# Router logits with transposed x as the stationary side

## What is computed

```python
h = modulate(rms_norm(x, norm2_g[i]), sh2, sc2)        # (256, 1024)
scores = sigmoid(h @ router_w)                         # (256, 16)
biased = scores + router_bias
# best group by the sum of its two best, best two experts in it, weights = scores / their sum
for e in range(16):
    y = y + gates[:, e:e+1] * (silu(h @ w1[e]) * (h @ w3[e]) @ w2[e])
x = x + g2 * y
```

## Time and profile before

| | |
|---|---|
| median of 3 runs | 1086.7 us (1086.18 to 1087.69) |
| span of the profiled execution | 1085.1 us |
| TensorE busy (PE) | 1046.2 us, 96% |
| weight loads (PEld) | 574.4 us, 53% |
| VectorE busy | 469.5 us, 43% |
| ScalarE busy | 174.3 us, 16% |
| read from HBM | 330.54 MB |

### The profile page before, as it was taken

How to read it: one execution, slowest core, us unless ns; L and a number is a source line. 1 busy time by engine, 2 the same in 40 slices (tenths; PEclk the granted TensorE clock), 3 DMA queues, 4 the chain that set the end, 5 groups by cost and what they waited for, 6 DMA issues and landing times.

```text
span 1085.1 us, 17591 instructions
## 1 busy us (share of the span) xinstructions
PE 1046.2 (96%) x7533; PEld 574.4 (53%) x7533; DVE 469.5 (43%) x1024; ACT 174.3 (16%) x340; POOL 20.4 (2%) x40
## 2 busy tenths in 40 slices
PE   7999999999999999999999999999999999999885
PEld 3688667654446344443448866765444634444322
DVE  3477696644125422352235769660112532222114
ACT  4021101310014113101121110031001410111102
POOL 3000000000000000000000000000000000000000
PEclk9999999999999999999999999999999999999998
DMA  9997846268953999999999884525665399999992
GB/s 305 391 386 256 304 157 214 79 216 321 413 229 135 411 420 415 421 421 420 421 398 368 295 301 166 185 89 194 252 266 217 137 422 421 420 421 421 421 420 118
DMA packets 90917, 332.78 MB, mean 307 GB/s; under 512 B 5020, under 2 KB 5355, under 8 KB 66005
## 3 DMA queue, kind: packets, MB, share of 16 engines
q1 hardware_dynamic: 87905, 323.56, 76.3%
q0 software_dynamic: 2048, 6.09, 1.6%
q10 hardware_dynamic: 884, 1.97, 0.6%
HBM read 330.54 MB, written 1.05 MB: 306 GB/s over the span
## 4 chain that ended last, share of the span: by engine, by line
PE 82%; DMA 7%; DVE 6%; SPq 3%; issue 1%; ACT 1%; DVEq 0%
PE bank L735 80%; DMA ring<-in_moe_w_dram 3%; SPq L665 2%; DMA wide<-in_moe_w_dram 2%; DMA ring<-in_w_ada_dram 2%; PE bank L1007 1%; PE bank L1175 1%; DVE wide L1586 0%; DVE area L1779 0%; DVE wide L1784 0%; DVE area L1782 0%; PE bank L1093 0%; DVE area L1781 0%; DVE area L1780 0%; PE bank L788 0%
## 5 line engine op out<-in xcount | busy, mean ns | idle before, releaser
L735 PE MATMUL bank<-ring,hT 128*32 128x512 f32 (+3 forms) x1808 | 311.6, 555 | 4.4 <-DMA ring<-in_moe_w_dram 1.8
L735 PE MATMUL bank<-hT,ring 128*32 128x256 f32 (+1 forms) x2112 | 214.1, 380 | 0.2 <-DVE hT L1620 0.2
L735 PEld LDWEIGHTS bank<-ring,hT 128*32 128x32 f32 (+2 forms) x1808 | 129.0, 136 | 152.8 <-issue 149.1
L735 PEld LDWEIGHTS bank<-hT,ring 128*32 128x32 f32 (+1 forms) x2112 | 158.7, 132 | 55.3 <-issue 8.7
L735 PE MATMUL bank<-area 32*64 32x64 f32 (+5 forms) x648 | 96.1, 363 | 0.5 <-ACT area L1468 0.5
L735 PE MATMUL bank<-ring,area 128*32 128x512 f32 x664 | 81.8, 594 | 0.5 <-ACT area L1468 0.5
L2051 DVE TENSOR_TENSOR area<-bank,area 128x512 f32<-128x512 f32 x14 | 9.7, 691 | 148.4 <-PE bank L735 148.4
L735 PEld LDWEIGHTS bank<-area 32*64 32x64 f32 (+4 forms) x648 | 43.8, 145 | 54.2 <-issue 52.2
L735 PE MATMUL bank<-wide,hT 128*32 128x512 f32 x368 | 65.9, 603 | 2.8 <-DMA ring<-in_moe_w_dram 1.4
L735 PE MATMUL bank<-ring,wide 128*128 128x512 f32 (+1 forms) x192 | 64.0, 597 | 0.8 <-DMA ring<-in_w_ada_dram 0.8
L1586 DVE SCALAR_TENSOR_TENSOR area<-ring,wide,area 128x512 f32<-128x512 f32 x84 | 63.1, 751 | 2.5
(11 more groups left out here) (266 smaller groups left out, 895.3 us busy)
## 6 DMA issues: line engine op xcount, KB each, us to landing
ring<-in_moe_w_dram SPq DMA_DIRECT2D x135, 1024.0 KB, 14.5
ring<-in_w_in_dram SPq DMA_DIRECT2D x26, 2048.0 KB, 11.4
ring<-in_w_ada_dram SPq DMA_DIRECT2D x24, 2048.0 KB, 14.2
wide<-in_moe_w_dram SPq DMA_DIRECT2D x33, 1024.0 KB, 12.2
cst<-in_moe_w_dram SPq DMA_DIRECT2D x13, 1024.0 KB, 14.9
area<-in_moe_w_dram SPq DMA_DIRECT2D x11, 1024.0 KB, 14.5
ring<-in_w_out_dram SPq DMA_DIRECT2D x4, 2048.0 KB, 8.0
ring<-in_w_br_h_dram SPq DMA_DIRECT2D x4, 1536.0 KB, 7.9
```

The source lines that it names most:

```text
L735: return pe.matmul(dst, lhsT, rhs, start=start, stop=stop, skip_group_check=True)
```

## The change

The partial sums, ScalarE's copy of them and the fold are taken out. `route(tt)` now makes, for each of the eight pieces, one matmul with the transposed x (128 tokens) as the stationary side and `routerA[:, k, :]` (16 columns, no zeros) as the moving side, all eight added up in 16 columns of bank 2. The result has the tokens on the rows. The wait for ScalarE's half of `xT` stands ahead of the fifth matmul. `routerA` is stored without padding and is no longer filled with zeros. The fillers stay as they are.

```diff
-        turned_in = region(ND * 32 + SEQ)
-        routerA = turned_in[:, 0:ND * 32].rearrange("p (k e) -> p k e", k=ND)
-        part = turned_in[:, ND * 32:].rearrange("p (t s) -> p t s", t=NT)
+        routerA = region(ND * NE).rearrange("p (k e) -> p k e", k=ND)
...
                 def route(tt):
-                    for r in range(2):
-                        if r == 0:
-                            pe.wait_ge(v_ra, L + 1)
-                            pe.wait_ge(v_xT, L * NT + tt + 1)
-                        else:
+                    pe.wait_ge(v_ra, L + 1)
+                    pe.wait_ge(v_xT, L * NT + tt + 1)
+                    for k in range(ND):
+                        if k == 4:
                             pe.wait_ge(a_xT, L * NT + tt + 1)
-                        for j in range(4):
-                            k = 4 * r + j
-                            last = mm(bank[tt][32 * j:32 * j + 32, 0:P], routerA[:, k, :], xT[:, tt, k, :],
-                                      r == 0, r == 1)
-                    last.then_inc(p_part, 1)
+                        last = mm(bank[2][:, tt * NE:(tt + 1) * NE], xT[:, tt, k, :], routerA[:, k, :],
+                                  k == 0, k == ND - 1)
+                    if tt == NT - 1:
+                        last.then_inc(p_lg, 1)
...
                 route(1)
-                for tt in range(NT):
-                    pe.wait_ge(a_part, L * NT + tt + 1)
-                    last = mm(bank[2][:, tt * NE:(tt + 1) * NE], part[:, tt, :], fold, True, True)
-                last.then_inc(p_lg, 1)
                 keep_clock(3, 9)
...
-                def keep_part(tt):
-                    sc.wait_ge(p_part, L * NT + tt + 1)
-                    sc.activation(part[:, tt, :], bank[tt][:, 0:P], ACT.Copy).then_inc(a_part, 1)
...
                 keep_xT(0)
-                keep_part(0)
...
                 keep_xT(1)
-                keep_part(1)
...
-                        link(dv.memset(routerA, 0.0))
-                        dv.tensor_tensor(routerA[:, :, 0:NE], router[:, :, :],
+                        dv.tensor_tensor(routerA, router[:, :, :],
```

More of the change, by code:

```diff
@@ L455, in trunk_kernel @@
         a_xT = sem("a_xT")
-        p_part = sem("p_part")
-        a_part = sem("a_part")
         v_lg = sem("v_lg")
```

## The result

The changed kernel takes 1089.45 us (median of 12 runs, 1088.47 to 1090.54), the kernel before beside it 1086.91 us (12 runs, 1086.18 to 1088.04): 2.54 us more, a ratio of 1.002 with a 95% interval of 1.0013 to 1.0027. The forecast was 1089.4 us. The profiled execution has a span of 1087.8 us.

A forecast was written before the change was run, and what follows sets the result against it. TensorE, on 82% of the chain that ended last, bounds the kernel; 2 layers x 1.37 = 2.75 us on the 1085.1 us span makes 1087.8, with 1.6 us outside it 1089.4 us; range 1087.0 to 1092.9.

The forecast's parts named there:

- the sum: Router delay over both layers: 2 x 1.37 = 2.75 us added to the kernel's time.
- The pace p: Time from one weight load to the next in the new route on TensorE: taken as 0.121 us.
- the stated bounds: Limits kept for the time between weight loads in the new route: 0.114 to 0.19 us.
- The sliced loads' 0.024: Load spacing of the old route's 32-column slices; as a rival for the new route, 1085.0 us, chance 0.05.
- 30p - 2.27: Delay of the router's sigmoid per layer, p being the time between weight loads: 1.37 us with p = 0.121.
- Part 1: route(0), ahead of turn_x(1) on TensorE: its loads and the four fillers start turn_x(1) 1.12 us later.
- Part 2: route(1), with copy and fold removed: the logits start at 339.49 us, 1.70 us later than before.
- Part 3: ScalarE's sigmoid table load: done before the logits, it gives back 0.33 us, so the sigmoid is 1.37 us later.
- Part 4: Behind the router: clock fillers end at 343.86 us, VectorE's release at 343.80, no idle time; TensorE about 1.39 us later.
- Parts at nothing: Removed memset and copies, SP's queue, GpSimd's filter-weight loads 1.7 us later, VectorE's reciprocal-root instructions: no effect on the time.
- The end: Expert stage behind the router: DMA is empty at 350 to 352 us, so the 1.4 us delay is carried along.
- Rival (c), the clock: TensorE's clock falls around the router: 3.4 us more at once per layer, 1092.8; once only 1091.1; chance 0.10.

The follow-up runs named there:

- the repeat: The changed kernel run once more, unaltered, beside the kernel before: 1089.21 us against 1086.97, ratio 1.0020.
- the run with a known delay: The kernel before with thirteen fillers instead of four between route(0) and turn_x(1): 1090.85 us against 1087.09, ratio 1.0036.
- the run with route(0) alone: The kernel before with only route(0) swapped to transposed x as stationary side, route(1) left in slices with copy and fold: 1088.99 us against 1086.97, ratio 1.0018.

## Why the prediction was right, and where it wasn't

**Direction, mechanism, size.** 1089.4 forecast, 1089.45 measured. The router by the trace costs 1.06 and 1.04 us; the forecast had 1.37 each. So the sum, 2.75 us, was 0.65 too high, and that the total met the median within 0.05 is luck: 0.44 us lies between the profiles' 2.10 and the runs' 2.54 (2.24 in the repeat), and 0.21 is the kernel before, 1086.91 beside the changed one and not 1086.7. The 2.10 lies inside the runs' interval (1.4 to 2.9 us), and I don't claim a cause for the 0.44.

**The pace p was mis-sized: 0.121 in place of 0.111.** I divided the time of eight loads by eight: 0.97/8. But such a row reaches to the end of the last load, which is 0.19 us long, so eight loads have seven steps: (0.97 - 0.19)/7 = 0.111. From one row's start to the next it is the same: 335.02 to 335.91 for eight. The gather's 3.65 us for 32 loads gives (3.65 - 0.19)/31 = 0.112, not 0.114. The supposed lower bound was the same mistake, and the true value lay outside the stated bounds. The sliced loads' 0.024 has it too: with a last load of 0.11 us it is (0.38 - 0.11)/15 = 0.018. All rows of full stationary had one pace, and the new rows have it too: (1.86 - 0.19)/15 = 0.111. With it the formula of the prediction, 30p - 2.27, gives 1.06 per layer, though two of its constants were off by as much in opposite directions, as parts 1 and 2 show. The Trainium skill, TensorE: Matmul & The Clock Gate, section LDWEIGHTS, has a weight load take its columns over 1.2, an estimate of 0.107 us for 128; the rows are 4% above.

**Part 1** held: the early first load, and 0.89 us of delay (1.12 forecast; 0.15 too much by p over 15 steps, 0.08 by the fillers' length, 0.89 and not 0.97). That the fillers stood in the way was right, as the run without them showed.

**Part 2** held with two small errors, 0.07 us together, that cancel the 0.08 of the fillers' length: from VectorE's copy to route(1) 0.11 us, not 0.06 (the kernel before already had 0.12, 336.11 to 336.23); from the last load to the logits 0.41, not 0.39. Logits 1.39 later, forecast 1.70.

**Part 3** held: 0.34 us back from the table load, forecast 0.33, and shown alone, in the trace, by moving a copy of the kernel before.

**Part 4** held: no idle time ahead of the position matmuls, fillers and VectorE's release (343.90) together.

**Parts at nothing** held as far as shown: the memset was back in the run with 64 columns and moved nothing; the later filter-weight loads of GpSimd were not tried.

**The end** held: the run with a known delay gave it back in full. Of the changed kernel's own 1.06 us in layer 0, 0.95 arrived at layer 1's router in one profile and 1.31 in the other.

**Rival (c), the clock, was taken too lightly.** It didn't happen in the changed kernel, nor with four short fillers fewer, but with six fewer it did; the changed kernel without the two alone was not run. My evidence against it, 4.4 us of one-column matmuls and transposes at the start with the clock kept, had no idle time inside; the router without the two fillers had 0.5 us. Whether this idle time, the matmuls missing in it or both decide wasn't separated. The price was about right: 1.5 us a layer by the trace, against 1.7 forecast.

## What to carry to other kernels

When a matmul's small side is swapped from stationary to moving, count the weight loads: here a full stationary side cost 0.111 us a record with 16, 64 or 128 columns moved over it, and a slice of 32 columns about 0.02. When an edit makes a step longer or shorter, look again at the fillers and waits beside it; here 0.9 of 1.06 us was filler that had lost its wait. And a pace is read from starts, or from a row's length less the last instruction, over one step fewer than the count.

## What the runs showed of the hardware that I had not expected

- Eight float32 matmuls with 128x128 stationary take 1.86 us of weight loads with 16 moving columns and with 64.
- In the changed kernel without the four fillers, two matmuls of 128 columns, in a wait where they cost nothing, kept the clock: without them TensorE fell to 1.2 GHz in both layers (0.50 to 0.59 granted in windows of 2 us) right behind a stretch of weight-bound matmuls with 0.5 us of idle time in it. That is much less idle time than the 2.71 us before the fall at 1012 us in the kernel before. The length of a wait alone doesn't tell: 2.22 us at 543 us in the run with route(0) alone was followed by a fall, 2.13 us at 1017 us in the kernel before was not (1.00 from 1018 to 1022).
- In the changed kernel's first profile the granted clock reads 1.00 from 4 to 18 us, but eight filler records at 11.64 take 3.78 us, against 1.99 later, and in the kernel before six at 5.45 take 2.93 under a reading of 1.00. In these first microseconds the records' own times are the better witness. That the engine was at 1.2 GHz there is a reading of them, not something the column shows.
